# A pre-norm whose scale and shift move from VectorE to ScalarE, with the first weight split and the bias stores put behind it

## The reference

```
def rms_norm(x, g):
    y = xf * lax.rsqrt(jnp.mean(xf * xf, axis=-1, keepdims=True) + EPS)
    return (y * g.astype(jnp.float32)).astype(x.dtype)

def modulate(h, shift, scale):
    return h * (1 + scale[:, None, :]) + shift[:, None, :]

def swiglu(h, w_gu, w_down):
    a, b = jnp.split(h @ w_gu, 2, axis=-1)
    return (jax.nn.silu(a) * b) @ w_down
...
mods = jax.nn.silu(c) @ w_ada + b_ada      # nine vectors of 1024
```

## Time and profile before

| what | value |
|---|---|
| time, median of 3 runs | 2343.94 us (2342.18 to 2349.77) |
| the profiled execution: its own time | 2343.94 us |
| the profiled execution: span | 2342.2 us |
| TensorE matmul busy | 95% of the span |
| VectorE busy | 50% |
| ScalarE busy | 32% |
| DMA, mean over the span | 100 GB/s |
| mean granted TensorE clock | 0.96 of full speed |

### The profile page before, as it was taken

One profiled execution on the slowest core, in us unless ns is written; L12 is line 12 of the kernel. 1 busy time (PEld: TensorE's weight loads), 2 busy tenths in 40 slices (PEclk: granted clock), 3 DMA queues, 4 the chain that ended last, 5 costly groups with the idle time before them and its releaser, 6 DMA issues.

```text
span 2342.2 us, 27670 instructions
## 1 busy us (share of the span) xinstructions
PE 2215.8 (95%) x10832; PEld 1797.9 (77%) x10832; DVE 1164.4 (50%) x1866; ACT 742.0 (32%) x1079; POOL 0.2 (0%) x4
## 2 busy tenths in 40 slices
PE   7999999999999999999999899888798999999997
PEld 5888888788877677788888788664388877888886
DVE  7655654654236744433433645664456545333334
ACT  3321112322324643422212432555333333322222
POOL 0000000000000000000000000000000000000000
PEclk9999999999999999999999899878898998999998
DMA  8554452223221122232232123200033211322222
GB/s 340 209 186 180 180 182 98 97 90 108 90 90 39 52 72 88 74 106 91 90 106 91 60 96 133 91 1 1 18 108 108 72 65 45 107 90 102 95 90 72
DMA packets 35313, 234.98 MB, mean 100 GB/s; under 512 B 4347, under 2 KB 4603, under 8 KB 7708
## 3 DMA queue, kind: packets, MB, share of 16 engines
q1 hardware_dynamic: 31968, 227.62, 27.4%
q10 hardware_dynamic: 3260, 6.19, 0.7%
HBM read 229.07 MB, written 4.72 MB: 100 GB/s over the span
## 4 chain that ended last, share of the span: by engine, by line
PE 88%; DVE 8%; ACT 3%; issue 1%; DMA 0%; ACTq 0%; DVEq 0%; SPq 0%
PE ps L444 85%; PE ps L643 2%; DVE w_lo L1267 1%; ACT w_hi L901 1%; DVE act_lo L1301 1%; DVE x L1319 1%; ACT pt L901 0%; DVE normed L1317 0%; ACT sc L901 0%; DVE act L1310 0%; DVE ada_acc L1398 0%; DVE normed L1310 0%; DVE act L1786 0%; ACT act_hi L901 0%; DVE sumsq L1284 0%
## 5 line engine op out<-in xcount | busy, mean ns | idle before, releaser
L444 PE MATMUL ps<-act_hi,w_hi 128*128 128x512 f32 x1856 | 734.6, 396 | 25.7 <-DVE act_lo L1301 6.7
L444 PE MATMUL ps<-act_hi,w_lo 128*128 128x512 f32 x1856 | 726.3, 391 | 0.0
L444 PE MATMUL ps<-act_lo,w_hi 128*128 128x512 f32 x1856 | 726.1, 391 | 0.0
L1267 DVE TENSOR_TENSOR w_lo<-raw,w_hi 128x2048 fp32r<-128x2048 f32 x172 | 393.8, 2289 | 105.2 <-ACT w_hi L901 99.9
L901 ACT ACTIVATE w_hi<-raw 128x2048 fp32r<-128x2048 f32 (+1 forms) x188 | 338.5, 1800 | 333.4 <-PE ps L444 329.4
L444 PEld LDWEIGHTS ps<-act_hi,w_hi 128*128 128x128 f32 x1856 | 350.8, 189 | 107.0 <-issue 18.0
L444 PEld LDWEIGHTS ps<-act_hi,w_lo 128*128 128x128 f32 x1856 | 350.6, 189 | 74.7
L444 PEld LDWEIGHTS ps<-act_lo,w_hi 128*128 128x128 f32 x1856 | 351.0, 189 | 72.5 <-issue 1.0
L444 PE MATMUL ps<-hid_hi,w_hi 128*128 128x512 f32 x656 | 260.1, 397 | 1.7 <-DVE hid_lo L1518 1.7
L444 PE MATMUL ps<-hid_hi,w_lo 128*128 128x512 f32 x656 | 258.5, 394 | 0.0
L444 PE MATMUL ps<-hid_lo,w_hi 128*128 128x512 f32 x656 | 256.6, 391 | 0.0
(11 more groups left out here) (279 smaller groups left out, 2028.7 us busy)
## 6 DMA issues: line engine op xcount, KB each, us to landing
raw<-in_weights SPq DMA_DIRECT2D x176, 1024.0 KB, 4.9
ada_raw<-in_ada SPq DMA_DIRECT2D x30, 1024.0 KB, 5.0
ada_slot<-in_ada SPq DMA_DIRECT2D x6, 1024.0 KB, 11.1
bias_rows<-biasrow ACTq DMA_DIRECT2D x8, 320.0 KB, 6.9
x<-in_x SPq DMA_DIRECT2D x1, 2048.0 KB, 16.3
table<-bias_rows ACTq DMA_DIRECT2D x1, 2048.0 KB, 8.0
result<-x SPq DMA_DIRECT2D x8, 256.0 KB, 2.0
consts<-in_consts SPq DMA_DIRECT2D x1, 1088.5 KB, 29.2
```

The source lines that it names most:

```text
L444: return nc.tensor.matmul(out, lhsT, rhs, start=start, stop=stop)
L1267: v.tensor_tensor(w_lo[k][:], raw[k][:], w_hi[k][:].bitcast(F32), ALU.subtract).then_inc(split_lo, 1)
```

## The change

ScalarE now applies gain and shift together: for a modulated pre-norm VectorE writes only `x` times the reciprocal root into `normed` (two buffers), and ScalarE computes `gain * normed + shift` twice, once rounded into `act_hi` and once in fp32 into `act32` (two buffers). VectorE's `low` becomes a plain subtraction. At the start, `lo(0, 0)` moves from before `modulation(0, 2)` to behind the whole first pre-norm; the eight bias stores move on ScalarE's queue from before its first pre-norm to behind it; and the wait for these stores moves from VectorE to ScalarE. The norms without a shift keep their instructions.

```
-            def prenorm(shift=None):
+            def prenorm(shift=None, gain=None):
                 for t in range(DT):
                     act.wait_ge(normed_ready, count["normed"] + 1)
                     count["normed"] += 1
                     if shift is None:
                         fn(act_hi[:, t, :], gained[t % 4]).then_inc(act32_ready, 1)
-                    else:
-                        fn(act_hi[:, t, :], gained[t % 4], ACT.Identity,
-                           bias=shift[:, t:t + 1]).then_inc(act32_ready, 1)
+                        continue
+                    kw = dict(scale=gain[:, t:t + 1], bias=shift[:, t:t + 1])
+                    fn(act_hi[:, t, :], normed[t % 2][:], ACT.Identity, **kw)
+                    fn(act32[:, t % 2, :], normed[t % 2][:], ACT.Identity, **kw).then_inc(act32_ready, 1)
...
             hi(0, 0)
+            act.wait_ge(mods_ready, 1)
+            prenorm(mods[:, 0:8], gains[:, 0])
             act.wait_ge(brow_copied, 8)
             for h in range(8):
                 act.dma_start(scratch[h], biasrow[h][:]).then_inc(brow_out, 16)
-            act.wait_ge(mods_ready, 1)
-            prenorm(mods[:, 0:8])
+            act.wait_ge(brow_out, 16 * 8)
             ffn(AT["ffn1"], x)
...
-            def prenorm(gain, shift=None):
+            def prenorm(name=None):
                 def low(t):
                     dve.wait_ge(act32_ready, count["act32"] - DT + t + 1)
-                    high = act_hi[:, t, :].bitcast(F32)
-                    if shift is None:
-                        ins = v.tensor_tensor(act_lo[:, t, :], gained[t % 4], high, ALU.subtract)
-                    else:
-                        ins = v.scalar_tensor_tensor(out=act_lo[:, t, :], in0=gained[t % 4],
-                                                     scalar=shift[:, t:t + 1], in1=high,
-                                                     op0=ALU.add, op1=ALU.subtract)
-                    ins.then_inc(act_ready, 1)
+                    whole = act32[:, t % 2, :] if name is None else gained[t % 4]
+                    v.tensor_tensor(act_lo[:, t, :], whole, act_hi[:, t, :].bitcast(F32),
+                                    ALU.subtract).then_inc(act_ready, 1)
                 for t in range(DT):
                     if t >= 2:
                         low(t - 2)
-                    v.scalar_tensor_tensor(out=gained[t % 4], in0=x[:, t, :], scalar=gain[:, t:t + 1],
-                                           in1=ps[:, 5, :], op0=ALU.mult,
-                                           op1=ALU.mult).then_inc(normed_ready, 1)
+                    if name is None:
+                        ins = v.tensor_tensor(normed[t % 2][:], x[:, t, :], ps[:, 5, :], ALU.mult)
+                    else:
+                        ins = v.scalar_tensor_tensor(out=gained[t % 4], in0=x[:, t, :],
+                                                     scalar=col(name, t), in1=ps[:, 5, :],
+                                                     op0=ALU.mult, op1=ALU.mult)
+                    ins.then_inc(normed_ready, 1)
...
-            lo(0, 0)
             modulation(0, 2)
             v.tensor_scalar(negsink[:], col("sinks", 0, 16), -1.0, None, ALU.mult)
             gain(0, 1, "g_ffn1").then_inc(mods_ready, 1)
-            dve.wait_ge(mods_ready, 1)
-            prenorm(gains[:, 0], mods[:, 0:8])
-            dve.wait_ge(brow_out, 16 * 8)
+            prenorm()
+            lo(0, 0)
             ffn(AT["ffn1"], gains[:, 3], ada=True)
```

More of the change, by code:

```diff
@@ L1054, in _ @@
             act.wait_ge(mods_ready, 2)
-            prenorm(mods[:, 24:32])
+            prenorm(mods[:, 24:32], gains[:, 1])
             for i in range(4):
@@ L1100, in _ @@
             take_root()
-            prenorm(mods[:, 48:56])
+            prenorm(mods[:, 48:56], gains[:, 2])
             ffn(AT["ffn2"], x)
@@ L1593, in _ @@
             invert()
-            dve.wait_ge(mods_ready, 2)
-            prenorm(gains[:, 1], mods[:, 24:32])
+            prenorm()
             for u in range(2):
@@ L1693, in _ @@
             invert()
-            prenorm(gains[:, 2], mods[:, 48:56])
+            prenorm()
             ffn(AT["ffn2"], gains[:, 4])
@@ L1705, in _ @@
             invert()
-            prenorm(col("mixpre", 0, DT))
+            prenorm("mixpre")
             link(v.memset(upad[:, :, 0:3], 0.0))
@@ L1908, in _ @@
                     invert()
-            prenorm(col("xpre", 0, DT))
+            prenorm("xpre")
             for q in range(4):
@@ L1926, in _ @@
             invert()
-            prenorm(col("fpre", 0, DT))
+            prenorm("fpre")
             ffn(AT["ffn3"], None)
```

## The result

The changed kernel took 2371.05 us (median of 4 runs, 2363.04 to 2376.18) against 2343.06 for the kernel before in the same comparison: a ratio of 1.0115, 95% interval 1.0092 to 1.0138, so it is slower, by a little over 1%. The forecast was 2360, with a range up to 2367. The profiled execution took 2373.09 us, with a span of 2371.2, 29.0 more than the span before.

What follows compares the result with a forecast made beforehand. TensorE, busy 95% of the span, was taken as the bound. Added to 2343.94 us, 11.9 for `lo(0, 0)` behind the first pre-norm and 4.1 for ScalarE's later end at the other two made 2360, range 2355 to 2367.

Steps and rivals of the forecast that it cites:

- the steps it summed: 11.9 us at the start plus 4.1 us at the second and third pre-norms, 16.0 us in all.
- Block 0: Start of ffn1: its first matmul waits for `lo(0, 0)` behind the first pre-norm, so begins at 61.7, not 48.76.
- Two pointer operands: ScalarE's activation in modulated pre-norms, with scale and bias pointers, takes 0.82 us; rival of a free second pointer had 0.15.
- a pair: ScalarE's two activations per pre-norm tile take 1.44 us; the other bound was 1.26.
- ScalarE's end: Second and third pre-norms: ScalarE finishes later, delaying `w_hi` and `w_lo` of block 1 by 2.0 and 2.1 us.
- the first block: Block 0 of ffn1 takes 12.5 us as before, so block 1 begins at 74.2, 11.9 us later.
- the stores: Bias stores behind the first pre-norm end at some 66 to 68, hidden by block 0, costing 0.
- The rival: Start: the stores end after 68.6 and hold block 1, 1.5 to 6.6 us more, 2361.5 to 2366.6; chance 0.17.
- The rival at ffn2: TensorE's idle time before block 1 grows to 3.2 us and its clock halves, 1.6 us more, 2361.6; chance 0.06.
- equal times in all other stretches: Sign in the profile: outside the start and the second and third pre-norms, stretches take the same time as before.
- the level that the sum was made against: The whole kernel before: its profiled execution's 2343.94 us, taken as the median too.
- the 7 us: Whole kernel: a measurement tells 0.3% (7 us) from no change; slower was given 0.94.

Runs made afterwards that it cites:

- after_stores_early: The changed kernel with the bias stores issued ahead of the first pre-norm again, `lo(0, 0)` late and the wait where the change put it; ratio 1.0093 to the kernel before.
- after_lo_early: The changed kernel with `lo(0, 0)` back in its old place; ratio 1.0085 to the kernel before.
- delay_norms: The kernel before with two small activations, some 2 us, on ScalarE at the end of each of the three modulated pre-norms; ratio 1.0054.
- affine_hi_early: The kernel before with ScalarE's two activations in the modulated pre-norms and `w_hi` of block 1 made before each pre-norm; ratio 1.0005.
- delay3: The kernel before with three chained memsets on VectorE ahead of its first pre-norm product, a pure delay; ratio 1.0006.
- lo_late: The kernel before with `lo(0, 0)` alone moved behind the first pre-norm; ratio 1.0037.
- delay_n2: The kernel before with 2 us of ScalarE work at the end of the second pre-norm alone, ahead of the convolution; ratio 1.002.
- delay_n3: The kernel before with 2 us of ScalarE work at the end of the third pre-norm alone, ahead of ffn2; ratio 1.003.
- affine_only: The kernel before with ScalarE's two activations in place of one in the three modulated pre-norms, all else as before; ratio 1.0047.
- affine_again: A second run of affine_only, the kernel before with ScalarE's two activations alone; ratio 1.004.
- stores_late: The kernel before with the bias stores and their wait alone moved behind ScalarE's first pre-norm; ratio 1.0044.

## Why the prediction was wrong

**Right.** The place and size of the steps it summed. Block 0 was forecast at 61.7 and began at 61.44. Two pointer operands were taken at 0.82 us and a pair at 1.44: the trace shows 0.81 and pairs every 1.42 to 1.45 (46.90 to 57.66, 15 steps of 0.717). ScalarE's end cost 1.98 at the second and at the third pre-norm, for 2.0 and 2.1, and reached block 1 mostly through `w_hi` and `w_lo`, as the runs with `w_hi` made ahead show. The steps add up to 17.9 us in the profile, for 16.0.

**A term mis-sized: the first block.** "It won't be shorter ... with a longer stretch without them I expect the same" held block 0 for 12.5 us. Counted in the same way it took 13.8 (61.44 to 75.42, less the overlap of 0.16), since the half clock lasted 6.1 us and not 3.1: 1.3 us. Part of that is the luck of one execution. After the same idle time block 0 took 13.5 in after_stores_early. And with the 3.0 us pause of the kernel before, the half clock lasted 3.1 to 5.2 us over the eight profiles that have this pause. So the length of the idle time alone does not set it; in the kernel before the granted clock was 0.57 on the mean from 41 to 46 us, so it had fallen ahead of that pause.

**A term that should not have been 0: the stores.** Costed at nothing "because the DMA queues are empty", with the wait ending at 66 to 68. It ended at 70.5. The text named block 2's load as joining at 61.6 and left out the modulation load behind it; the pair cost the stores 5.3 us, which after_lo_early shows. Since block 0 ran long by itself, only 0.8 of it came through. The rival had the mechanism right; its 1.5 to 6.6 was counted from a block 0 that ends at 74.2.

**The rival at ffn2 happened as well** in the profiled execution, at 1.5 for its price of 1.6. But its condition did not: TensorE's idle time did not grow to 3.2 us, it was 2.05, less than the 2.33 that the kernel before went through at full clock. What made the clock fall is open.

**The step that failed** is the last one: "equal times in all other stretches", and with it the level that the sum was made against. From the fifth to the sixth norm, in the mLSTM stage, the changed kernel took 10.2 us longer than the profile of before, at a mean clock of 0.67 in place of 0.94 in those 60 us. No case of the forecast reached beyond the stages that the change touches. Without these 10.2 us the profiled execution would have ended near 2363, inside the range.

The level was off too. The kernel before has slower executions as well, a third of them; that these are slow in the same stage is likely but not shown. Its own scatter, 2339 to 2359, is wider than the 7 us that the forecast called enough to tell from no change. Against the mean of all 134 executions the changed kernel's 23 are 23.2 us slower: 17.9 of delays, and 5.3 that these do not explain. Two groups are visible in the kernel before, with means of 2344.8 and 2354.9. That 16 of 23 executions are in the slower one and not 42 of 134 gives some 3.9 us, an estimate from these numbers. Half clock at the second and third norm, which cost 3.0 us in the profile, can be the rest.

**What raises that share** is suggested, not shown. It goes with block 1 of ffn2 coming 2 us later after the first product (55 of 77 against 57 of 182). It is not the two activations as such: delay_norms has none of them and was high six times of six, affine_hi_early has them and was above 2352 once in twelve. Nor is it a shift in time (delay3, lo_late), nor 2 us behind the second pre-norm (delay_n2). But only delay_n3 singles out the third pre-norm, with 7 of 12 against 4 of 12 in delay_n2 on the same chip; their means are 4.2 us apart with a standard error of 2.3, and chance is not ruled out. How something at 957 comes to matter at 1640 stays open: in the profiles of affine_only and affine_again block 1 of ffn2 ran at full clock, and the stretch was slow all the same, and in lo_late and stores_late it was slow with block 1 of ffn2 in its old place.

## What to carry to other kernels

Ahead of a pause of TensorE, ask which split or copy of the next block stands behind the norm on its engine, and do it before the norm: this took out three pauses here, and covered 3.9 of the 5.9 us that ScalarE's extra work had cost in the three norms. Two late things at the start cost little more than the later one, but they can meet in the DMA queues: list what each released load will share the queue with. And where parts of a kernel have thin TensorE work, take many executions of the kernel before as the level before judging half a per cent: here four of them had a median of 2343, and 134 a mean of 2348.

## What the runs showed of the hardware

An activation of 512 elements takes 0.63, 0.725 and 0.81 us with no, one and two pointer operands, and in the last case the next one begins 0.72 us after it. Eight stores of 320 KB to device memory from an empty queue were over 8.3 us after the first issue, and 13.6 with two 1 MB loads issued 4.6 us behind the first. Block 0 at the start began at half clock in every profile. With 3.0 us without a matmul ahead of it this lasted from 3.1 us (before) to 5.2 (delay_n3), with 13.9 us 4.8 (lo_late), with 15.7 us 5.3 and 6.1 (after_stores_early and the changed kernel). The granted clock in the table of stretches reads 1.00 for the last of these (61.4 to 67), where the steps of 0.43 us say half, so at the beginning of a trace the steps are the surer reading.
